# LoRA gates and the transposed V computed in bulk during the projection and re-read chunk by chunk, in a one-core RWKV-7 / convolution mixer layer

## What is computed

```python
h = rms_norm(x, g_pre) * (1.0 + scale) + shift
z = h @ w_in                                   # 1024 -> 4096, split into za, zb, zc, gc
...                                            # branch A: width-3 conv; branch B: width-31 conv, LayerNorm
zc = centred_shift(zc, mu)                     # p + mu * (0.5 * (prev + next) - p)
r, k, v, lw, la = split(zc)                    # 512, 512, 512, 2*64, 2*64 channels
wl = w0 + einsum('btdr,drc->btdc', tanh(lw), w2)     # LoRA's second product, decay, 2 directions
decay = exp(-exp(-softplus(-wl) - 0.5))
a = sigmoid(a0 + einsum('btdr,drc->btdc', la, a2))   # LoRA's second product, rate
kk = l2norm_per_head(k * k_k);  kd = k * (1.0 + (a - 1.0) * k_a)
s_fwd, y_fwd = rwkv7_scan(s0_fwd, r, decay[0], kd[0], v, kk, a[0], False)
s_bwd, y_bwd = rwkv7_scan(s0_bwd, r, decay[1], kd[1], v, kk, a[1], True)
...                                            # bonus, group norm, SiLU gates
out = concat(ya, yb, yc) @ w_out;  x = x + gate * rms_norm(out, g_post)
```

## Time and profile before

| | |
|---|---|
| median of 3 runs | 1130.68 us |
| the profiled execution: time, and its span | 1131.15 us, 1129.3 us |
| granted TensorE clock, mean | 0.955 |
| PE busy | 1018.8 us, 90% |
| DVE / ACT / POOL busy | 646.2 / 426.8 / 407.0 us |
| DMA | 61.46 MB, queue q1 at 14.8% of 16 engines |

### The profile page before, as it was taken

How to read it: one execution, slowest core, us unless ns; L and a number is a source line. 1 busy time by engine, 2 the same in 40 slices (tenths; PEclk the granted TensorE clock), 3 DMA queues, 4 the chain that set the end, 5 groups by cost and what they waited for, 6 DMA issues and landing times. The chain is left out here.

```text
span 1129.3 us, 32050 instructions
## 1 busy us (share of the span) xinstructions
PE 1018.8 (90%) x14407; PEld 916.6 (81%) x14407; DVE 646.2 (57%) x954; ACT 426.8 (38%) x708; POOL 407.0 (36%) x372
## 2 busy tenths in 40 slices
PE   5699998999789999994599999999999998779997
PEld 3399997999779988983599988999999997447685
DVE  5430019678564222243678878888888884365532
ACT  5351111101133333222355655566556552533311
POOL 7121220311104413321545545566666663232110
PEclk9799998999899999996599999999999998989999
DMA  9612332111102300000000000000000000641131
GB/s 360 239 38 75 117 117 75 38 38 38 38 3 86 108 6 32 1 1 10 1 3 4 4 13 4 4 4 4 4 3 5 3 4 3 242 170 48 64 112 56
DMA packets 30036, 61.46 MB, mean 54 GB/s; under 512 B 3352, under 2 KB 21444, under 8 KB 28748
## 3 DMA queue, kind: packets, MB, share of 16 engines
q1 hardware_dynamic: 29900, 59.42, 14.8%
HBM read 49.68 MB, written 9.73 MB: 53 GB/s over the span
## 5 line engine op out<-in xcount | busy, mean ns | idle before, releaser
L682 PE MATMUL ps<-input_rounded,weights_rounded 128*128 128x386 f32 x768 | 265.4, 346 | 10.6 <-DVE zc L888 6.0
L684 PE MATMUL ps<-input_rounded,weights_rest 128*128 128x386 f32 x768 | 261.4, 340 | 0.0
L683 PE MATMUL ps<-input_rest,weights_rounded 128*128 128x386 f32 x768 | 261.0, 340 | 0.0
L1403 POOL TENSOR_TENSOR arena<-arena,lvl 128x512 f32<-128x512 f32 x108 | 138.2, 1294 | 78.0 <-ACT arena L1320 46.8
L682 PEld LDWEIGHTS ps<-input_rounded,weights_rounded 128*128 128x128 f32 x768 | 146.1, 190 | 18.4 <-issue 9.3
L471 POOL TENSOR_TENSOR weights_rest<-arena,weights_rounded 128x2048 fp32r<-128x2048 f32 x16 | 75.3, 4707 | 218.9 <-ACT weights_rounded L516 218.9
L683 PEld LDWEIGHTS ps<-input_rest,weights_rounded 128*128 128x128 f32 x768 | 146.0, 190 | 0.7 <-issue 0.3
L684 PEld LDWEIGHTS ps<-input_rounded,weights_rest 128*128 128x128 f32 x768 | 146.0, 190 | 0.0
L1119 PE MATMUL ps<-arena 64*64 64x64 f32 x2880 | 107.7, 225 | 17.8 <-issue 14.6
L1119 PEld LDWEIGHTS ps<-arena 64*64 64x64 f32 x2880 | 95.8, 139 | 23.6 <-issue 17.1
L1129 PE MATMUL ps<-arena 64*64 64x64 f32 x2880 | 107.0, 226 | 4.4 <-DVE arena L1529 4.1
(11 more groups left out here) (241 smaller groups left out, 1721.4 us busy)
## 6 DMA issues: line engine op xcount, KB each, us to landing
arena<-in_w_in SPq DMA_DIRECT2D x16, 1024.0 KB, 5.3
arena<-in_ada_w SPq DMA_DIRECT2D x7, 1024.0 KB, 5.2
mix_scratch<-zc SPq DMA_DIRECT2D x4, 1158.0 KB, 9.3
out<-arena SPq DMA_DIRECT2D x9, 512.0 KB, 2.6
zc<-in_x_sample SPq DMA_DIRECT2D x4, 1024.0 KB, 8.8
hT<-in_ada_w SPq DMA_DIRECT2D x4, 1024.0 KB, 12.0
zc<-in_w_out SPq DMA_DIRECT2D x4, 1024.0 KB, 8.2
arena<-in_x_sample SPq DMA_DIRECT2D x8, 512.0 KB, 3.5
```

The lines of the kernel that those rows point to most:

```text
L682: pe.matmul(o, w_hi[:, k, cut], hi_of_h[:, k, cols_b], start=(k == 0), stop=False)
L683: pe.matmul(o, w_hi[:, k, cut], lo_of_h[k][:, cols_b], start=False, stop=False)
L684: last = pe.matmul(o, w_lo[:, k, cut], hi_of_h[:, k, cols_b], start=False, stop=(k == KT - 1))
L1403: pool.tensor_tensor(Um[l % 3], UT, lvl[:, l, :].unsqueeze(1).to_broadcast([P, 2 * PAIRS, C]), ALU.mult).then_inc(q_um[l], 1)
```

## The change

Both second products of the LoRA run in the projection for all 1158 columns: 24 parts of two matmuls (64 x 128 x 386), from mix tile 3 to 9, behind a cut of a tile, with two parts at three of the places. ACT applies tanh with the bias folded in, DVE the last scale and shift, and SP stores the result to a scratch tensor in device memory. V is transposed in mix tiles 10 to 13 (36 transpositions of 128 x 128 in 12 groups) and stored by token. In the scan SP loads for each chunk decays and rates (two DMAs each) and V (four DMAs) into two buffers each, decays and rates two chunks ahead. The mix tiles come in the order lw/la, k, v, r. `kk_norm` moves two tiles forward. The gate tiles are spilled with piece 3, and the table of taps is heavier at its start. In the scan the four engines' orders are rewritten: PE drops `lora` and `transpose_v`, puts `transpose_keys` behind level 4's product and `rhs_begin` ahead of level 5's, POOL and ACT change the order of masks, copies and key factors.

```diff
-          ("mix", 7), ("mix", 8), ("mix", 9), ("mix", 10), ("mix", 11), ("mix", 12), ("mix", 13)]
+          ("mix", 13), ("mix", 9), ("mix", 10), ("mix", 11), ("mix", 12), ("mix", 7), ("mix", 8)]
+MIX_AT = [12, 13, 4, 5, 6, 7, 8, 9, 10, 11, 0, 1, 2, 3]
+K0, V0, R0 = (MIX_AT.index(m) for m in (4, 8, 0))
+LORA0 = 3
+    LORA_AT[(LORA0 + _n // NB, _n % NB)] = 2 if _n in (7, 13, 19) else 1
+LORA_STORES = [(0,), (1, 2), (3, 4), (5, 6, 7)]
...
# SP, projection
-                    if (kind, k) == ("z", 4):
+                    if (kind, k) == ("z", 3):
                         spill(4, T[:, 4:6, :], s_gc, 2, s_sg)
-                    if (kind, k) == ("z", 5):
                         spill(6, T[:, 6:8, :], s_gc, 4, s_sg)
+                            sp.wait_ge(s_lf, 2 * (q + 1))
+                            for d in range(2):
+                                sp.dma_start(lora_dram[which, d, :, a, :], lora_out[q % 2][:, d, :]).then_inc(s_ld[q % 2], 16)
...
# ACT, projection
+                def lora():
...
+                        if q >= 2:
+                            act.wait_ge(s_ld[q % 2], 32 * (q // 2))
+                    act.wait_ge(s_lp, at + 1)
+                    for d in range(2):
+                        act.activation(lora_out[q % 2][:, d, n * NC:(n + 1) * NC], ps[:, 6 + d, 0:NC], ACT.Tanh, scale=0.5,
+                                       bias=col(("w0", "a0")[which], 4 * d + a)).then_inc(s_lz, 1)
...
# PE, projection
+                def lora():
...
+                    if at:
+                        pe.wait_ge(s_lz, 2 * at)
+                    pe.wait_ge(*kk_free())
+                    for d in range(2):
+                        r = slice(64 * d, 64 * d + 64)
+                        last = pe.matmul(ps[:, 6 + d, 0:NC], (w2s, a2s)[which][r, P * a:P * a + P],
+                                         (lwm, lam)[which][r, n * NC:(n + 1) * NC], start=True, stop=True)
+                def kk_free():
+                    return (s_kd, NB * kk_done[0]) if kk_done[0] else (s_yb, 1)
...
# DVE, projection
-                taps_after = dict(zip(range(U1, MIX0), (5, 6, 6, 6, 7, 7, 3, 3, 6, 6, 4, 3)))
+                taps_after = dict(zip(range(U1, MIX0), (8, 8, 8, 8, 7, 7, 3, 3, 4, 3, 2, 1)))
...
# SP, scan
+                def load_v(n):
+                    earlier(sp, q_state, n - 1)
+                    earlier(sp, q_yb, n - 1)
...
+                            sp.dma_start(UV[n % 2][OTHER[d], d, h:h + PAIRS, :], rows[:, g]).then_inc(q_vl[n % 2], 16)
+                for n in range(N):
+                    load_v(n)
+                    if n + 2 < N:
+                        load_decays(n + 2)
+                        load_rates(n + 2)
...
# ACT, scan: v_by_token, decay_tanh, decay_shift, rate_tanh and rate are gone
+                        keys_by_token(n2)
                         copy_y(n2, 2)
                         copy_y(n2, 3)
                     if 0 <= n1 < N:
-                        keys_by_token(n1)
+                        gather_triangle(n1)
+                    if 0 <= n0 < N:
+                        key_factor(n0)
...
# POOL, scan
+                        mask_level(n3, 0)
+                        mask_level(n3, 1)
+                        mask_level(n3, 3)
+                        mask_level(n3, 4)
+                        mask_level(n3, 2)
+                    if 0 <= n2 < N:
+                        keys_over_decay(n2)
+                        bonus_keys(n2)
+                    if 0 <= n4 < N:
+                        decay_state(n4)
                     if 0 <= n1 < N:
+                        b_keys(n1)
```

More of the change, by code:

```diff
@@ L68 @@
 MIXES = TILES.count("mix")
+MIX_AT = [12, 13, 4, 5, 6, 7, 8, 9, 10, 11, 0, 1, 2, 3]
+K0, V0, R0 = (MIX_AT.index(m) for m in (4, 8, 0))
+LORA0 = 3
+LORAS = [(which, a) for which in range(2) for a in range(4)]
+LORA_PARTS = [(q, n) for q in range(len(LORAS)) for n in range(NB)]
+LORA_AT = {}
+for _n in range(NB * (R0 - LORA0)):
+    LORA_AT[(LORA0 + _n // NB, _n % NB)] = 2 if _n in (7, 13, 19) else 1
+assert sum(LORA_AT.values()) == len(LORA_PARTS)
+LORA_STORES = [(0,), (1, 2), (3, 4), (5, 6, 7)]
+V_GROUPS = [(a, g) for a in range(4) for g in range(3)]
 RING = 3
@@ L283, in hybrid_step_kernel @@
         s_lwt = sem1("lw_tanh_ready")
+        s_lp = sem1("lora_multiplied")
+        s_lz = sem1("lora_tanh_ready")
+        s_lf = sem1("lora_finished")
+        s_ld = [sem1(f"lora_stored_{h}") for h in range(2)]
+        s_vp = sem1("v_transposed")
+        s_vs = [sem1("v_by_token_even"), sem1("v_by_token_odd")]
+        s_vd = [sem1(f"v_stored_{h}") for h in range(2)]
         s_cv = sem1("conv_b_done")
@@ L555, in _, with beside @@
                 round_weights(1)
+                def beside(j, b):
+                    for _ in range(LORA_AT.get((j - MIX0, b), 0)):
+                        lora()
+                    at = NB * (j - MIX0 - R0) + b
+                    if at >= 0 and at % 2 == 0:
+                        v_by_token(at)
                 for j, kind in enumerate(TILES):
+                    beside(j, 0)
+                    beside(j, 1)
                     h, z = j % 2, zbanks(j)
@@ L688, in _ @@
                         layer_norm(NB * (j - MIX0) + b)
-                    if MIX0 + 6 <= j <= MIX0 + 9 and b == 0:
-                        kk_norm(j - MIX0 - 6)
+                    if MIX0 + K0 + 2 <= j <= MIX0 + K0 + 5 and b == 0:
+                        kk_norm(j - MIX0 - K0 - 2)
+                    for _ in range(LORA_AT.get((j - MIX0, b), 0)):
+                        lora()
+                    if j >= MIX0 + R0:
+                        transpose_v(NB * (j - MIX0 - R0) + b)
                     if b < NB - 1:
@@ L868, in layer_norm, with lora, v_by_token @@
                                                  op0=ALU.mult, op1=ALU.mult).then_inc(s_yb, 1)
+                lora_done = [0]
+                def lora():
+                    q, n = LORA_PARTS[lora_done[0]]
+                    which, a = LORAS[q]
+                    lora_done[0] += 1
+                    if n == NB - 1:
+                        dve.wait_ge(s_lz, 2 * lora_done[0])
+                        for d in range(2):
+                            o = lora_out[q % 2][:, d, :]
+                            if which == 0:
+                                dve.tensor_scalar(o, o, 1.0, None, ALU.add).then_inc(s_lf, 1)
+                            else:
+                                dve.tensor_scalar(o, o, 0.5, 0.5, ALU.mult, ALU.add).then_inc(s_lf, 1)
+                def v_by_token(at):
+                    a, g = V_GROUPS[at]
+                    if g < 2:
+                        if a < 2:
+                            dve.wait_ge(s_ld[0], 16 * len(LORAS))
+                        else:
+                            dve.wait_ge(s_vd[a % 2], 32)
+                    n = min(4, 9 - 4 * g) * P
+                    dve.wait_ge(s_vp, at + 1)
+                    dve.tensor_copy(zc[:, 16 + a % 2, 512 * g:512 * g + n], ps[:, 6 + at % 2, 0:n]).then_inc(s_vs[at % 2], 1)
                 def kk_ready():
@@ L875, in kk_ready, with beside @@
                                                  in1=ps[:, 6 + at % 2, 0:NC], op0=ALU.mult, op1=ALU.mult).then_inc(s_kn, 1)
+                def beside(j, b):
+                    for _ in range(LORA_AT.get((j - MIX0, b), 0)):
+                        lora()
+                    at = NB * (j - MIX0 - R0) + b
+                    if at >= 0 and at % 2 == 1:
+                        v_by_token(at)
                 for j, kind in enumerate(TILES):
+                    beside(j, 0)
+                    beside(j, 1)
+                    if j == len(TILES) - 1:
+                        beside(j, 2)
                     h, z = j % 2, zbanks(j)
@@ L1070, in _ @@
             def _(pe):
-                def lora(n):
-                    earlier(pe, q_kv, 2 * n)
-                    for which, (w, src) in enumerate(((w2s, lwT), (a2s, laT))):
-                        for a in range(PAIRS):
-                            for d, r in enumerate(HALVES):
-                                at = C * (PAIRS * which + a)
-                                last = pe.matmul(ps[:, 4 + d, at:at + C], w[r, P * a:P * a + P],
-                                                 src[r, STARTS[n][d]:STARTS[n][d] + C], start=True, stop=True)
-                    last.then_inc(q_lora, 1)
-                def transpose_v(n):
-                    earlier(pe, q_m[1], 2 * n)
-                    for d in DIRS:
-                        for a, g in HEADS:
-                            last = pe.matmul(ps[OTHER[d], 6 + (g ^ d), C * a:C * a + C], chunk(vT, n, d)[HALVES[g], a, :],
-                                             eyes[HALVES[g], :], start=True, stop=True)
-                    last.then_inc(q_vt, 1)
                 def gram(n, d):
@@ L1386, in _ @@
                     pool.memset(LS[:, :, :, at:at + 1], 0.0)
-                    pool.memset(xw[:, :, :, at:at + 1], 0.0)
+                    for tile in TW:
```

(1 more changed line is left out.)

343 lines of the change are left out of this document (189 added, 154 removed).

## The result

| | before | after |
|---|---|---|
| median of 5 runs each | 1130.52 us (1130.20 to 1131.49) | 1137.16 us (1136.32 to 1140.26) |
| ratio, 95% interval | | 1.0062 (1.0048 to 1.0077) |
| SP's first DMA of the scan | 516.08 | 544.40 |
| chunk 0's first gram | 539.70 | 559.15 |
| chunk 2's first gram | 589.58 | 605.84 |

The account below looks back on a forecast made before the run. PE was taken to bound projection and scan, with DVE close behind in the scan. Scan -36 and projection +30.6 made -5.4 on the profiled 1131.15 us, so a median of 1125 us, faster, range 1107 to 1141.

Parts of the forecast that it names:

- A step of 20.95, a gain of 1.55: Steady scan: PE sheds 2.82 us per step, some returns as waits; step falls from 22.5, 23 us over 15 steps.
- DVE's order sets the step: Rival, scan: queries, level 2's transpose and factors 4 and 5 on DVE hold PE; step 21.7, 1136 us; chance 0.20.
- The ramp: Scan's start up to chunk 0's gram: the first cumulated sum needs only its load, so 9 us earlier.
- the projection: Projection: LoRA, waits and V add 37.8 us, waits that go take off 7.2; +30.6, from +17 to +46.
- a part 1.03: Projection: each of 24 LoRA parts costs PE three pass lengths, 0.98 us, and 0.05 for a switch.
- the GLU's -6.0: Projection: PE's wait of 6.0 us for DVE's GLU goes, because the spill comes with piece 3.
- the LayerNorm's -1.2: Projection: PE's 5.9 us wait for the last taps before the LayerNorm shrinks by 1.2 (0 to 5.9).
- The end, +1: Scan's last two steps: rhs_begin stands ahead of level 5's product and its factor is open, +1 us.
- Late chunk loads: Rival, scan: chunk loads in runs of 256 bytes come late; a 1 us wait per step makes 1143; chance 0.04.
- No overlap of pairs: Rival, projection: LoRA's matmul pairs on the two row halves don't overlap, +8 us, 1133; chance 0.12.
- full shedding: Rival, scan: PE stays packed and sheds 2.7 us per step, 17 us more, 1108; chance 0.10.
- a cheaper projection: Rival, projection: pairs overlap fully and the LayerNorm's wait goes whole, -12 us, 1113; chance 0.09.

Follow-up runs that it names:

- DVE's two places: Changed kernel, one DVE edit each: level 1's transpose ahead of the keys, 1129.75 us; factor 5 ahead of the next chunk's first transpose, 1130.44 us.
- the kernel with the early spill: Kernel before, with only the gate tiles spilled with piece 3 and the new table of convolution taps: 1118.25 us (0.9903).
- POOL and DVE in better order: Changed kernel with POOL's masks as before, its keys moved, level 1's transpose ahead of keys, b_over_decay behind level 2's transpose: 1109.60 us (0.9821).

## Why the prediction was wrong

- **What bounds the scan: the failed step.** "A step of 20.95, a gain of 1.55" was mis-sized; over 15 steps it was 22.20 and a gain of 0.33, 18.8 us less before rounding. What failed is the overlap it counted on: it let PE wait 1.80 per step, and PE waited 3.05. By these waits, in the mean of the 15 steps: update 5 waited 1.05 instead of 0.4 (+0.65), level 2's product 1.17 instead of 0 (+1.17), level 3's product 0.53 instead of 0.70 (-0.17), update 4 0.30 instead of 0.45 (-0.15), and the 0.25 added for small waits weren't needed. +1.25 together, and 15 x 1.25 is the 18.8.
- Two causes, both readable in the orders before the run. The forecast noticed that POOL slows the queries and applied it only there; it left `begin_inverse` at its 0.69 although POOL's mask 1, moved up, now follows mask 0 without a pause, and factor 5 stands behind it. And it followed DVE's new order at levels 4, 5 and 3, but not at level 1, where `keys` had gone ahead of the transpose and `b_over_decay` ahead of factor 2. Putting back POOL's order and moving its keys is worth 19.2 us by the experiment, more than the 18 that were missing; masks back in their old order, with nothing else, are worth 9.5, and DVE's two places 7.4 and 6.7, each alone.
- **The rival "DVE's order sets the step"** came nearest: it named 21.7 and 1136 us, measured 22.2 and 1137. It had 0.20. That DVE sets the step was right, but its time was partly luck: it named levels 3, 4 and 5 and not level 2's product, with 1.17 the largest wait, it missed POOL's share, and the better end made up for the longer step. And "it loses four ops" did not speak against it: what counts is what stands ahead of one factor or transpose.
- The ramp (-9, measured -8.9), the projection (+30.6, measured +28.3) and its parts (a part 1.03, measured 0.85 to the next group and some 0.2 in the first matmuls around it; the GLU's -6.0, the LayerNorm's -1.2, measured -1.3) were right or near. (24 x 1.03 is 24.7 and not 24.5; nothing hangs on it.) The reason given for 1.03, three passes in a row, was wrong: by the two sizes measured it is 1.7 lengths of columns and 0.36 besides, so a cost that is right to a tenth or two came from a wrong split. Of ACT's tables only the load itself shows: it takes 1.28 us from 364.06, and the root begins at 365.36.
- The end, +1, measured -4.9: the forecast took the clock as it was. That the fall to 1.2 GHz cost the kernel before some 3.5 us there follows from the kernel with the early spill, whose code there is the same and whose clock stayed up; what sets the fall off is open. The rest, 1.4, may be `outputs_begin` and the masks; it wasn't tried.
- Late chunk loads (0.04): out. No overlap of pairs, full shedding, a cheaper projection: none of them. With POOL and DVE in better order the step is 20.39, nearer to full shedding's 19.7 than the forecast's 20.95.
- That the final state's turn costs 0.8 us after (22.40 - 21.63) and 3.2 before (25.43 - 22.19) was not foreseen. After, it stands where PE waits anyway; this is argued from its place.

## What to carry to other kernels

When work leaves the busiest engine, list for the next engine what stands ahead of every result that the first one waits for, at every level and not only at the places that had a gap before. Lay the other elementwise engine's list beside it: two that both work on SBUF tiles must be placed in time together, and an idle slot on one is worth nothing if it is the other's busy one. And undo the parts of a bundled change one by one: here the small part (a spill one and two pieces earlier) was worth 12 us alone, and a reordering of POOL 19. A kernel in which the clock falls in a stretch where PE has little work can carry 1.5 to 3.5 us that have nothing to do with an edit; compare such a stretch by itself.

## What the runs showed of the hardware

- `begin_inverse`, one 128x512 subtraction with both inputs in SBUF, takes 0.65 us alone and 1.30 behind a POOL multiplication of 1.25 that began 0.5 earlier. The cumulated sum takes 1.24 alone and 2.37 beside three masks, and those masks then take 1.56 each instead of 1.27. DVE's masks, which read PSUM, kept 678 to 693 ns in the steady scan of every kernel, beside POOL or not. The Trainium skill (SBUF — State Buffer, Who interferes with whom) says that a DVE instruction with two inputs in SBUF contends with a GpSimd instruction that reads SBUF, that the port pair which they share is an exclusive lock, and that the order of issue decides who blocks. The subtraction agrees: mask 1 began at about 832.54 and ended at 833.79, and a wait until then plus 0.65 ends at 834.44, where 834.34 was measured. For the sum and the masks, both slowed, no run here separates such turns from a shared rate.
- Pairs of fp32 matmuls on the two halves of the rows overlap: a part of four passes took 0.92 us with 386 columns and 0.41 with 32. Taken as even growth, that is an estimate of 1.7 pass lengths for the columns and 0.36 us besides; what the 0.36 are made of isn't shown.
- 144 loads in runs of 256 bytes, 64 and 128 KB each at 2.4 and 3.0 us, cost the scan nothing: 1136.94 us without those of 16 chunks, 1137.16 with them, and steps of 21.6 and 22.6 in both.
- The same code behind gram 17 took 42.3 us in one build, with the granted clock at 0.5 from about 952 to 962 us, and 38.7 in another with the clock at 1.00 throughout.
